# One engine program for the first layer's recurrence and its output product, the last head written out, and VectorE's key norm moved ahead in the second layer's first steps

## The chip, the cores and the metric

The kernel runs on one core of a Trainium2 chip. The time is the device time of one execution in microseconds (us), and shorter is better. Three runs of the kernel before took 2409.99, 2412.68 and 2415.59 us, so their median is 2412.68 us. The engines are TensorE (PE; the loading of its weights is listed apart as PEld), VectorE (DVE), ScalarE (ACT), GpSimd (POOL) and SyncE (SP), which here only issues transfers.

## The reference, cut to what matters

Three layers follow one another on x of 1024 rows by 1024 columns, all in float32: a retention layer, a window attention layer and a layer of two attention branches. The change touches the first layer and the first steps of the second.

```python
def retention_layer(x, g_norm, w_in, w_out, sin, cos):
    proj = rmsnorm(x, g_norm) @ w_in
    q, k, v, gate = jnp.split(proj, [...], axis=-1)      # 4 heads, q and k 256 wide, v and gate 512 wide
    q, k = theta_shift(q, sin, cos), theta_shift(k, sin, cos)
    o = rms(retention(q, k, v))                          # 8 chunks of 128 rows, a state carried from one to the next
    o = o.reshape(b, s, RET_V_TOTAL) * jax.nn.silu(gate) # 1024 x 2048
    return x + o @ w_out                                 # 2048 x 1024

def shared_kv(x, g_norm, w_kv, g_k):                     # head of the second layer
    kv = rmsnorm(x, g_norm) @ w_kv                       # 1024 x 256
    k, v = jnp.split(kv, [KV_WIDTH], axis=-1)
    k = rmsnorm(k, g_k)                                  # by head of 64
```

## The kernel before, in words

Rows are worked in 8 tiles of 128 (index t). Every large product is made of three TensorE matmuls, because each float32 operand is split into a high part (written by ACT) and a low part (the rest, written by DVE): high by high, low by high, high by low. So a product over 1024 rows of weights and 512 columns is 24 matmuls of 128x512, and a block of weights can be used only once ACT and DVE have split it. There is no planner: each engine's order is written out by hand, an engine works its own list from top to bottom, and semaphores join the lists. A wait holds up all that stands behind it in the same list.

**`retain` (L195).** After a preamble that makes the transposed normed rows hT, a loop on each engine (`Fori`) runs over the 4 heads. In each head there are three passes over the 8 tiles: queries with keys, values, gates. The third pass (the `for t in range(TILES)` in each engine's program) also does the recurrence: TensorE transposes the tile's queries and keys (L376), makes half of the gate product, the scores, the state's increment, the second half of the gate product, and last the tile's output into bank `p_o` (L275). ACT takes the square sum of that output (L507), POOL its power (L325), DVE multiplies output, factor and gate into `o_gated` (L652), and ACT stores these 128x512 rows to `ret_o_dram` (L455). While heads run, `w_raw` (the memory of `early_w_kv`) takes the next half block of weights and ACT and DVE split it (L420, L521) into `w_first` (one pair for each pass) or `w_second` (shared). At the end of the last head, this brings in the first block of the output weights: its upper half is split after tile 4, the lower half after tile 7.

**`retention_product` (L659).** It is a `Block` of its own, with memory, banks and semaphores of its own, entered once all engines have left `retain` and its semaphores are cleared. It loads the 2048 wide rows of tile t back from `ret_o_dram` (tile 0 to `o_rows`, tile 1 to `o_second`, which is the memory of `x_rows`; L712), transposes them in 16 pieces on TensorE (`transpose_rows`, L763), splits them in four steps on ACT (L808) and DVE (L850) to `oT`, and multiplies (`product(t, half)`, L780, 48 matmuls). It needs four blocks of output weights in the order of use: the one that `retain` left, one through `raw` (2 MB, L713, k of 0 to 7 for the left half of the columns), one in two halves through `raw_half` (1 MB each, L714 and L721, k of 8 to 15 for the right half), one through `raw` again (L719). ACT (L800) and DVE (L864) split them in this order, counted in `w_lo`. TensorE's list begins so:

```python
            transpose_rows(0)
            transpose_rows(1)
            for t in range(0, TILES, 2):
                product(t, 0)
                product(t + 1, 0)
                product(t, 1)
```

Here `product(0, 0)` waits for `w_lo` of 8 before its k of 0, and `product(0, 1)` for 16 at its start and 24 before its k of 0. DVE adds the product to the rows of x (L857).

**`window_layer` (L885), its first steps.** TensorE works in steps s: `rows(s)` transposes the rows of a tile (L1107), `keys_values(s - 1)` makes keys and values of the tile before (24 matmuls of 128x256), `transpose_keys(s - 2)` transposes the normed keys (L1122), which `norm_keys` on DVE has written to `kn` (L1426). DVE's list for a step is: `norm_low(s)` (two low parts of hT, L1411), `scale_rows(s + 3)` (rows times their factor, L1400, which waits for their load), `norm_keys(s - 2)`, `key_squares(s - 1)` (L1421), in steps 0 to 3 two `split_low` (L1417) and one `flip_bias` (L1405). Between `key_squares` and `norm_keys` of a tile lie a small ACT instruction (L1267) and POOL's power (L1068).

## Time and profile before

| | |
|---|---|
| median of three runs | 2412.68 us (2409.99 to 2415.59) |
| the profiled execution | 2418.01 us, of which the span of instructions is 2416.2 us |
| instructions | 33085 |
| share of the span: DVE, ACT, POOL busy | 46%, 37%, 9% |
| mean granted clock of TensorE | 0.976 of full speed |

The retention layer's heads run to 702 us of the span, the output product to 912 us and the second layer's key steps to some 970 us. Times in the rows are microseconds from the span's start. A busy share near 100% on one engine says that this engine is never without work in that stretch; an idle time stands in brackets with what ended it. The granted clock is the share of full speed at which TensorE was let run.

### The profile page before, as it was taken

The page shows a single profiled execution, that of the slowest core. Times are in us where ns is not written, and L with a number is a line of the kernel's source. Part 1 is how long each engine was busy: PE and PEld are TensorE (multiplying, and loading weights), DVE is VectorE, ACT ScalarE, POOL GpSimd, SP SyncE. Part 2 cuts the span into 40 slices and gives each one's busy share as a digit, 9 for nine tenths or more (in the row PEclk, how much of TensorE's full clock was granted, in tenths as well). Part 3 has the DMA queues.
Part 4 walks back from the last instruction along what each step waited for, and adds up shares of the span by engine and source line. Part 5 has one row for each costly group of instructions (what it writes and reads, how often), then busy time and mean ns, then how long its engine had stood idle before and what let it go on. Part 6 is the DMA issues. An engine that isn't in the chain of part 4 may idle for free. (4 is left out here: it accounts for less than half of the span.)

```text
span 2416.2 us, 33085 instructions
## 1 busy us (share of the span) xinstructions
PE 2281.6 (94%) x11898; PEld 1829.1 (76%) x11898; DVE 1116.9 (46%) x3122; ACT 885.2 (37%) x2276; POOL 212.3 (9%) x315
## 2 busy tenths in 40 slices
PE   6999999999979998999989799999999999799998
PEld 5888888888867887677767686777777777688876
DVE  5255264253453124445453316566665766533342
ACT  4142242341343113455543214454544544423232
POOL 1000000000000000112110000010010101101013
PEclk9999999999989999999999899999999999899999
DMA  4111111111136113011133501110111102424322
GB/s 142 38 53 52 54 56 50 56 48 54 48 132 220 70 61 114 10 49 51 49 109 107 171 34 58 60 43 8 60 43 60 44 7 77 131 73 122 96 96 87
DMA packets 125284, 174.95 MB, mean 72 GB/s; under 512 B 7576, under 2 KB 73176, under 8 KB 123616
## 3 DMA queue, kind: packets, MB, share of 16 engines
q1 hardware_dynamic: 119088, 157.39, 19.8%
q10 hardware_dynamic: 6064, 15.84, 1.8%
q8 instruction: 78, 1.28, 0.2%
q14 instruction: 54, 0.44, 0.1%
HBM read 143.79 MB, written 29.42 MB: 72 GB/s over the span
## 5 line engine op out<-in xcount | busy, mean ns | idle before, releaser
L91 PE MATMUL heads_p_ps<-ret_w_second_hi_sb,ret_hT_hi_sb 128*128 128x512 f32 x384 | 150.8, 393 | 1.8 <-DVE ret_w_second_lo_sb L521 1.8
L91 PE MATMUL heads_p_ps<-ret_w_second_lo_sb,ret_hT_hi_sb 128*128 128x512 f32 x384 | 149.8, 390 | 0.0
L91 PE MATMUL heads_p_ps<-ret_w_second_hi_sb,ret_hT_lo_sb 128*128 128x512 f32 x384 | 149.4, 389 | 0.0
L91 PE MATMUL att_proj_ps<-br_w_second_hi_sb,br_hT_hi_sb 128*128 128x512 f32 x272 | 117.3, 431 | 2.8 <-DVE br_w_second_lo_sb L2193 2.8
L2149 ACT ACTIVATE br_x_sb<-br_x_sb,att_max_neg_sb 128x256 f32<-128x256 f32 (+7 forms) x128 | 97.8, 767 | 27.4 <-DVE att_max_neg_sb L2366 27.3
L91 PE MATMUL att_proj_ps<-br_w_second_lo_sb,br_hT_hi_sb 128*128 128x512 f32 x272 | 107.1, 394 | 0.0
L91 PE MATMUL att_proj_ps<-br_w_second_hi_sb,br_hT_lo_sb 128*128 128x512 f32 x272 | 106.8, 392 | 0.0
L91 PEld LDWEIGHTS heads_p_ps<-ret_w_second_hi_sb,ret_hT_hi_sb 128*128 128x128 f32 x384 | 72.1, 188 | 18.8 <-issue 3.9
L2635 ACT ACTIVATE mrg_yT_hi_sb<-br_y_raw_sb 128x1024 fp32r<-128x1024 f32 x32 | 33.9, 1060 | 140.6 <-PE mrg_b_ps L2566 120.2
L91 PEld LDWEIGHTS heads_p_ps<-ret_w_second_lo_sb,ret_hT_hi_sb 128*128 128x128 f32 x384 | 72.1, 188 | 15.6
L91 PEld LDWEIGHTS heads_p_ps<-ret_w_second_hi_sb,ret_hT_lo_sb 128*128 128x128 f32 x384 | 72.2, 188 | 15.2
L2566 PE MATMUL mrg_b_ps<-mrg_w_br_hi_sb,mrg_yT_hi_sb 128*128 128x256 f32 x256 | 74.1, 289 | 9.6 <-DVE mrg_w_br_lo_sb L2727 8.1
L91 PE MATMUL swa_p_ps<-swa_w_first_hi_sb,swa_hT_hi_sb 128*128 128x512 f32 x160 | 70.9, 443 | 10.5 <-DVE swa_qn_sb L1441 7.0
L1974 PEld LDWEIGHTS att_t_ps<-all_ident_sb,br_x_sb 128*128 128x128 f32 x432 | 47.4, 141 | 41.2 <-DVE br_x_sb L2383 20.4
L1974 PE MATMUL att_t_ps<-all_ident_sb,br_x_sb 128*128 128x128 f32 x432 | 66.6, 281 | 9.5 <-DVE br_x_sb L2383 7.8
L420 ACT ACTIVATE ret_w_second_hi_sb<-early_w_kv_sb 128x512 fp32r<-128x512 f32 x52 | 28.5, 621 | 126.7 <-PE heads_p_ps L91 126.7
L2749 DVE TENSOR_TENSOR mrg_sig_sb<-mrg_b_ps,mrg_sig_sb 128x512 f32<-128x512 f32 x32 | 22.1, 689 | 113.2 <-PE mrg_b_ps L2566 113.2
L325 POOL TENSOR_TENSOR heads_o_rstd_sb<-heads_o_ms_sb,heads_minus_half_sb 128x1 f32<-128x1 f32 x32 | 17.6, 551 | 645.6 <-ACT heads_o_ms_sb L509 645.6
L2566 PE MATMUL mrg_b_ps<-mrg_w_br_lo_sb,mrg_yT_hi_sb 128*128 128x256 f32 x256 | 73.3, 286 | 0.0
L2566 PE MATMUL mrg_b_ps<-mrg_w_br_hi_sb,mrg_yT_lo_sb 128*128 128x256 f32 x256 | 73.2, 286 | 0.0
L857 DVE TENSOR_TENSOR early_x_rows_sb<-ret_out_y_ps,early_x_rows_sb 128x512 f32<-128x512 f32 x16 | 10.9, 688 | 129.8 <-PE ret_out_y_ps L780 129.8
L479 ACT ACTIVATE heads_v_sb<-heads_p_ps 128x512 f32<-128x512 f32 x32 | 19.2, 598 | 140.2 <-PE heads_p_ps L91 140.1
(472 smaller groups left out, 6553.0 us busy)
## 6 DMA issues: line engine op xcount, KB each, us to landing
early_w_kv_sb<-a_w_blocks SPq DMA_DIRECT2D x28, 1024.0 KB, 5.3
all_w_block_sb<-w_turns SPq DMA_DIRECT2D x12, 2048.0 KB, 9.0
br_y_raw_sb<-branch_yT_dram SPq DMA_DIRECT2D x32, 512.0 KB, 4.0
ret_o_dram<-early_x_rows_sb ACTq DMA_DIRECT2D x32, 256.0 KB, 2.4
all_w_block_sb<-swa_turns SPq DMA_DIRECT2D x4, 2048.0 KB, 9.6
ret_out_o_rows_sb<-ret_o_dram ACTq DMA_DIRECT2D x6, 1024.0 KB, 6.0
x_dram<-early_x_rows_sb SPq DMA_DIRECT2D x12, 512.0 KB, 2.8
heads_v_sb<-x SPq DMA_DIRECT2D x8, 512.0 KB, 4.6
```

What stands on the lines that cost most here:

```text
L91: mm = pe.matmul(out, rows[a], w[b], start=(k == 0 and a + b == 0), stop=(k == KT - 1 and b == 1))
L325: pool.tensor_tensor(o_rstd[:, t % 2:t % 2 + 1], o_ms[:, t % 2:t % 2 + 1], minus_half[:], ALU.pow).then_inc(orstd_done, 1)
L420: act.activation(w_at(kind)(k)[0], w_raw[:, k % HALF, :], ACT.Copy).then_inc(w_hi, 1)
L479: act.activation(v[:, t, :], p_proj[t % 2][:], ACT.Copy).then_inc(v_copied, 1)
L857: dve.tensor_tensor(x_rows[:, t % 2, cols], p_y[t % 2][half][:], x_rows[:, t % 2, cols], ALU.add).then_inc(x_added, 1)
L1974: tr = pe.transpose(p_tr[b][:, j * P:(j + 1) * P], probs[:, t % 2, a, (lo + j) * P:(lo + j + 1) * P], ident[:])
L2149: act.activation(part, part, ACT.Exp, bias=max_neg[:, t % 2, a:a + 1], scale=SCALE, accum_out=p_sum[:, t % 2, a:a + 1]).then_inc(exp_done, 1)
L2566: mm = pe.matmul(p_br[b][:, n * QW:(n + 1) * QW], rows[i], w[j], start=(k + i + j == 0), stop=(k == PAIRS - 1 and j == 1))
L2635: act.activation(y_parts[t % 2][0][:], y_raw[:, t % RAWS], ACT.Copy).then_inc(y_hi, 1)
L2749: dve.tensor_tensor(sig[:, t % 2, :], p_br[t % 2][:], sig[:, t % 2, :], ALU.mult).then_inc(prod_done, 1)
```

## The change

It has two parts.

**One program for recurrence and product.** `retention_product` makes no block, banks or memory of its own any more. It returns one function for each engine, and `retain` calls them behind its heads. The loop over heads covers three heads, and the last is written out:

```diff
+        def last_heads(eng, body):
+            with eng.Fori(0, RET_HEADS - 1) as h:
+                body(Place(h, 1, 0))
+            body(Place(None, 0, RET_HEADS - 1))
...
+            last_heads(pe, head_pe)
+            out["pe"](pe)
```

In the last head's last tile the transposes of the product's tile 0 stand inside the recurrence, two quarters at a time, with the ACT and DVE parts that belong to them:

```diff
                     mm.then_inc(s_done, 1)
+                    if last and t == TILES - 1:
+                        out["pe_ahead"](pe, 0)
...
                     project(2, t, range(HALF, KT))
+                    if last and t == TILES - 1:
+                        out["pe_ahead"](pe, 1)
...
-                pe.wait_ge(gate_done, head.times(TILES, TILES))
+                if not last:
+                    pe.wait_ge(gate_done, head.times(TILES, TILES))
```

ACT's first part (`act_ahead`, 0) stands after its split of the decayed queries, the second after the gate of tile 7 and the store of tile 6. DVE's (`dve_ahead`) stands right before the wait of the last `gated`. In the last head ACT and DVE no longer wait for all stores of `o_gated`.

SP's list behind the last head, where each load waits for the recurrence's own semaphores. `rows_stored` is the store of the tile's rows for all four heads; `first_rows_free` is the output of tile 3 of the last head, `second_rows_free` the last value product; `raw_free` is the transposes of tile 7; `raw_half_free` is the recurrence's last split; `gated_free` is that all rows are stored:

```diff
+    def sync_program(sp):
+        for t, place, free in ((0, o_rows, "first_rows_free"), (1, o_second, "second_rows_free")):
+            frees["rows_stored"](sp, t)
+            frees[free](sp)
+            sp.dma_start(place[:], o_dram[t * P:(t + 1) * P, :]).then_inc(o_first[t], 16)
+        frees["raw_free"](sp)
+        sp.dma_start(raw[:], dram["a_w_blocks"][FIRST + 2].rearrange("(k p) n -> p k n", p=P)).then_inc(raw_in, 16)
+        frees["raw_half_free"](sp)
+        sp.dma_start(raw_half, weight_rows(dram, FIRST + 1, 0)).then_inc(half_in, 16)
+        frees["gated_free"](sp)
+        for t in range(2):
+            sp.dma_start(x_rows[:, t], dram["x"][0, t * P:(t + 1) * P, :]).then_inc(x_in[t], 16)
+        sp.wait_ge(w_lo, KT)
...
```

TensorE's order in the product begins anew (`order` is k of 8 to 15, then 0 to 7), and the transposes go through the banks of `p_o0`, `p_kv0`, `p_kv1`, `p_p0` in the order 2, 3, 0, 1:

```diff
-            transpose_rows(0)
-            transpose_rows(1)
-            for t in range(0, TILES, 2):
+        product(0, 0, order[0:HALF])
+        transpose_rows(pe, 1)
+        product(0, 0, order[HALF:KT])
+        product(1, 0, order[0:KT])
+        product(0, 0, order[KT:])
+        product(1, 0, order[KT:])
+        for t in range(0, TILES, 2):
+            if t:
                 product(t, 0)
                 product(t + 1, 0)
```

ACT's list behind the last head is the load of tile 2's rows, the copies of tile 1, then the 24 splits; DVE's is the low parts of tile 1, then the 24 splits. From `product(0, 1)` on, the lists are those of before. The buffers of the product now lie over buffers of the recurrence (`o_rows` over the first half of v, `o_second` over `w_v_lo`, `oT` over v, the queries and keys, `spare` and the state), for which the buffers of `retain` are put in another order; `x_more` and `w_kv_high` lie over `v_high`.

**DVE's order in the second layer's first steps.**

```diff
             for s in range(TILES + 2):
+                if s >= 2:
+                    norm_keys(s - 2)
                 if s < TILES:
                     norm_low(s)
-                if s + 3 < TILES:
-                    scale_rows(s + 3)
-                if s >= 2:
-                    norm_keys(s - 2)
+                if s == 0:
+                    scale_rows(3)
                 if 1 <= s <= TILES:
                     key_squares(s - 1)
+                if 2 <= s < TILES - 2:
+                    scale_rows(s + 2)
```

## Rows read from the trace of the kernel before

**Rows 1.** The page, busy time of an engine (share of the span) and its instructions

```profile
PE 2281.6 (94%) x11898; PEld 1829.1 (76%) x11898; DVE 1116.9 (46%) x3122; ACT 885.2 (37%) x2276; POOL 212.3 (9%) x315
```

**Rows 2.** Busy time by stretch: length, each engine's busy us (instructions), granted clock, DMA share, GB/s

```profile
592.00:702.00 110.00, 109.81 (x512) 90.43 (x511) 48.95 (x101) 41.27 (x93) 3.86 (x7) 1.00 0.13 45
702.00:722.00 20.00, 6.84 (x31) 6.05 (x30) 6.75 (x11) 6.61 (x13) 0.65 (x2) 0.58 0.64 235
722.00:750.00 28.00, 24.91 (x105) 20.18 (x104) 15.87 (x27) 13.84 (x26) 0.00 (x0) 0.94 0.60 218
750.00:912.00 162.00, 162.00 (x766) 135.47 (x764) 29.91 (x51) 22.91 (x46) 6.05 (x14) 1.00 0.28 101
917.00:975.00 58.00, 48.14 (x320) 44.33 (x319) 27.71 (x52) 22.17 (x60) 6.46 (x9) 0.91 0.33 110
```

**Rows 3.** Timeline of TensorE, 702 to 750 us: start, length, instruction [idle before]

```profile
702.03 0.39 PE L275 MATMUL heads_o_ps<-heads_state_lo_sb,heads_qdT_hi_sb 128*128 128x512 f32 x1
...
714.08 3.68 PE L763 MATMUL ret_out_t_ps<-all_ident_sb,ret_out_o_rows_sb 128*128 128x128 f32 x16 [11.65 <-DMA ret_out_o_rows_sb<-ret_o_dram]
719.26 3.31 PE L763 MATMUL ret_out_t_ps<-all_ident_sb,early_x_rows_sb 128*128 128x128 f32 x16 [1.50 <-DVE ret_out_oT_lo_sb L850]
722.32 0.47 PE L780 MATMUL ret_out_y_ps<-ret_w_qk_hi_sb,ret_out_oT_hi_sb 128*128 128x512 f32 x1
...
731.13 0.50 PE L780 MATMUL ret_out_y_ps<-ret_hT_hi_sb,ret_out_oT_hi_sb 128*128 128x512 f32 x1 [3.09 <-DVE ret_hT_lo_sb L864]
...
749.18 0.39 PE L780 MATMUL ret_out_y_ps<-ret_w_v_hi_sb,ret_out_oT_hi_sb 128*128 128x512 f32 x1
```

**Rows 4.** Timeline of the other engines' lists, 680 to 745 us

```profile
680.75 0.37 SPq L306 DMA_DIRECT2D early_w_kv_sb<-a_w_blocks  x1
...
704.04 0.75 DVE L652 SCALAR_TENSOR_TENSOR early_x_rows_sb<-heads_o_ps,heads_o_rstd_sb,heads_gate_sb 128x512 f32<-128x512 f32 x1 [5.51 <-POOL heads_o_rstd_sb L325]
704.71 2.49 DVE L521 TENSOR_TENSOR ret_w_second_lo_sb<-early_w_kv_sb,ret_w_second_hi_sb 128x512 fp32r<-128x512 f32 x4
...
709.54 0.43 SPq L713 DMA_DIRECT2D all_w_block_sb<-a_w_blocks  x1
...
726.17 4.91 DVE L864 TENSOR_TENSOR ret_hT_lo_sb<-all_w_block_sb,ret_hT_hi_sb 128x512 fp32r<-128x512 f32 x8 [2.16 <-ACT ret_hT_hi_sb L800]
...
731.11 0.38 SPq L719 DMA_DIRECT2D all_w_block_sb<-a_w_blocks  x1
733.52 0.38 SPq L721 DMA_DIRECT2D early_w_kv_sb<-a_w_blocks  x1
...
742.63 2.19 ACT L800 ACTIVATE ret_w_gate_hi_sb<-early_w_kv_sb 128x512 fp32r<-128x512 f32 x4 [10.76 <-DMA early_w_kv_sb<-a_w_blocks]
```

**Rows 5.** The tile of the product's transposes: duration ns min/median/max, first and last start

```profile
L850 DVE TENSOR_TENSOR ret_out_oT_lo_sb<-ret_out_t_ps,ret_out_oT_hi_sb x32: 681/681/693, 715.9 to 870.0; 128x512 fp32r<-128x512 f32 x32
```

**Rows 6.** The chain that ended last: start, length of 24 matmuls 512 and 256 wide

```profile
2140.20 5.49 PE mrg_g_ps L91 x24
2145.70 2.88 PE mrg_b_ps L2566 x24
```

**Rows 7.** Timeline of DVE, POOL and TensorE in the second layer's first steps

```profile
925.28 0.75 DVE L1400 TENSOR_SCALAR ret_out_x_more_sb<-ret_out_x_more_sb,early_rstd_sb 128x1024 f32<-128x1024 f32 x1 [1.34 <-DMA ret_out_x_more_sb<-x_dram]
...
926.62 0.70 POOL L1068 TENSOR_TENSOR swa_k_rstd_sb<-swa_k_ms_sb,swa_minus_half_sb 128x2 f32<-128x2 f32 x1 [9.80 <-ACT swa_k_ms_sb L1267]
...
929.05 1.28 DVE L1411 TENSOR_TENSOR swa_hT_lo_sb<-swa_s_ps,swa_hT_hi_sb 128x512 fp32r<-128x512 f32 x2
...
930.90 0.42 DVE L1426 TENSOR_TENSOR swa_kn_sb<-swa_o_ps,swa_k_rstd_sb 128x256 f32<-128x256 f32 x1
...
931.38 0.69 PE L1122 MATMUL swa_o_ps<-all_ident_sb,swa_kn_sb 128*128 128x128 f32 x2 [4.29 <-DVE swa_kn_sb L1426]
...
953.82 1.04 PE L1107 MATMUL swa_s_ps<-all_ident_sb,early_x_rows_sb 128*128 128x128 f32 x8
```

**Rows 8.** Busy time by stretch, as in rows 2, behind the wait for the first keys

```profile
934.00:936.00 2.00, 2.00 (x12) 2.00 (x11) 2.00 (x4) 0.41 (x1) 0.00 (x0) 0.50 0.58 188
```

More of the change, by code:

```diff
@@ L265, in w_at @@
+        banks = dict(tr=[p_p0, p_o0, p_kv0, p_kv1], y=[[p_tr, p_s], [p_p1, p_o1]])
+        out = retention_product(nc, mem, layer, ident, dram, early, hT, w_first, w_second, o_dram, banks, frees, minus_half)
         def w_at(kind):
@@ L493, in _ @@
                         act.activation(qdT[0][:, b], qkT[:, b, 0:2], ACT.Copy).then_inc(qd_hi, 1)
+                    if last and t == TILES - 1:
+                        out["act_ahead"](act, 0)
                     if t + 1 < TILES:
@@ L505, in _ @@
                         store_rows(t - 1)
+                    if last and t == TILES - 1:
+                        out["act_ahead"](act, 1)
                     act.wait_ge(o_done, head.times(TILES, t + 1))
@@ L513, in _ @@
                 store_rows(TILES - 1)
-            for b in range(2):
-                act.wait_ge(o_out[b], 16 * RET_HEADS * TILES // 2)
+            last_heads(act, head_act)
+            out["act"](act)
         @block.vector
@@ L656, in _, with retention_product @@
                 split_next(2, 1)
-                for b in range(2):
-                    dve.wait_ge(o_out[b], head.times(16 * TILES // 2, 16 * TILES // 2))
-def retention_product(nc, ident, dram, early, hT, w_first, w_second, o_dram):
+                if not last:
+                    for b in range(2):
+                        dve.wait_ge(o_out[b], head.times(16 * TILES // 2, 16 * TILES // 2))
+            last_heads(dve, head_dve)
+            out["dve"](dve)
+def retention_product(nc, mem, layer, ident, dram, early, hT, w_first, w_second, o_dram, banks, frees, minus_half):
     HALF = KT // 2
@@ new lines, in retention_product @@
+    raw = early["w_q0"]
+    raw_half = early["w_kv"][:].rearrange("p k n -> p (k n)").rearrange("p (k n) -> p k n", n=BANK)
+    o_rows = mem.over("v", "o_rows", P, RET_HEADS * RET_V)
+    o_second = layer.over("w_v_lo", "o_second", P, RET_HEADS * RET_V)
+    oT = [[mem.over("spare", "oT0_hi", P, KO, P, dt=F32R), mem.over("state", "oT0_lo", P, KO, P, dt=F32R)],
+          [mem.over("v", "oT1_hi", P, KO, P, dt=F32R, further=4 * RET_HEADS * RET_V), mem.over("qkT", "oT1_lo", P, KO, P, dt=F32R)]]
@@ L769, in product, with pe_ahead, pe_program @@
+    def pe_ahead(pe, part):
+        transpose_rows(pe, 0, ORDER[2 * part:2 * part + 2])
+    def pe_program(pe):
+        order = list(range(KT, KO)) + list(range(KT))
+        def product(t, half, ks=order):
+            if ks[0] == KT:
+                pe.wait_ge(oT_lo, 4 * t + (4 if t else 2))
                 if t >= 2:
                     pe.wait_ge(x_added, 2 * (t - 2) + half + 1)
-                for n, k in enumerate(order):
-                    if t == 0 and half == 0 and k == 0:
-                        pe.wait_ge(w_lo, KT)
-                    if t == 0 and half == 1 and n == 0:
-                        pe.wait_ge(w_lo, 2 * KT)
-                    if t == 0 and half == 1 and k == 0:
-                        pe.wait_ge(w_lo, 3 * KT)
-                    w = w_at(k, half)
-                    for a, b in ((0, 0), (1, 0), (0, 1)):
-                        mm = pe.matmul(p_y[t % 2][half][:], oT[t % 2][a][:, k, :], w[b],
-                                       start=(n == 0 and a + b == 0), stop=(n == KO - 1 and b == 1))
@@ L782, in product @@
-                mm.then_inc(y_done[half], 1)
-            transpose_rows(0)
-            transpose_rows(1)
-            for t in range(0, TILES, 2):
+                else:
+                    frees["bank_free"](pe, t, half)
+            for k in ks:
+                if t == 0 and half == 0 and k in (KT, KT + HALF):
+                    frees["early_w"](pe, HALF if k == KT else KT)
+                if t == 0 and half == 0 and k == 0:
+                    pe.wait_ge(oT_lo, 4)
+                    pe.wait_ge(w_lo, KT)
+                if t == 0 and half == 1 and k == KT:
+                    pe.wait_ge(w_lo, 2 * KT)
+                if t == 0 and half == 1 and k == 0:
+                    pe.wait_ge(w_lo, 3 * KT)
+                w = w_at(k, half)
+                for a, b in ((0, 0), (1, 0), (0, 1)):
+                    mm = pe.matmul(p_y[t % 2][half][:], oT[t % 2][a][:, k, :], w[b],
+                                   start=(k == KT and a + b == 0), stop=(k == KT - 1 and b == 1))
```

417 lines of the change are left out of this document (224 added, 193 removed).

## The prediction

> **What bounds the kernel now.** The page's busy times come first: TensorE is busy 2281.6 us of the span, 94% [rows 1], so what can be won is mostly its idle time and the time at half clock. The busy time by stretch says where these are [rows 2]. In the last head TensorE is busy 109.81 of 110 us at full clock, and in the steady product 162.00 of 162. Between them, from 702 to 722 us, it is busy 6.84 of 20 at a granted clock of 0.58, and from 722 to 750 24.91 of 28 at 0.94. In the second layer's first steps it is busy 48.14 of 58 at 0.91. The change works on these holes only.
>
> The timeline of TensorE shows the first hole from within [rows 3]. The recurrence's last matmul starts at 702.03, the rows' transposes only at 714.08, ended by the load of rows, and the first product matmul at 722.32. Both sets of 16 transposes run cold, at 3.68 and 3.31 us. A second wait of 3.09 us ends at 731.13 with the split of the third weight block, and `product(0, 1)` starts at 749.18. The other lists say why [rows 4]: behind the last split (704.71 and 2.49 us) all engines leave the program, SP issues the 2 MB of `raw` at 709.54, and its split on DVE starts at 726.17. In the second layer [rows 7] TensorE waits 4.29 us, until 931.38, for keys that DVE writes at 930.90, though POOL had their factor at 927.3 (926.62 and 0.70); behind that wait the clock is 0.50 [rows 8].
>
> **Part one: the seam.** I walk TensorE's new list in the clock of before. 24 matmuls 512 wide take 5.49 us at full clock [rows 6], so 12 take 2.75. Sixteen transposes take 3.68 us at half clock [rows 3]; at full clock I take half, 1.84.
>
> - The tile 0 transposes now stand inside the last tile of the last head and add 1.84 us. What they wait for is early: SP comes to the row loads right behind its last weight load, at 681.1 (680.75 and 0.37) [rows 4], some 16 us before the first transpose. The last recurrence matmul moves from 702.03 to 703.9, and all that hangs on it moves with it: the last split on DVE ends at 704.71 + 2.49 + 1.84 = 709.05 [rows 3, 4].
> - 704.1: `product(0, 0)` with k of 8 to 11, 2.75, to 706.85. Its low parts came from DVE while the gate product ran. Then tile 1's transposes, 1.84, to 708.7. Their rows were loaded with the first.
> - k of 12 to 15 need the last split, 709.05: a wait of 0.4. To 711.85.
> - `product(1, 0)` with k of 8 to 15 needs tile 1's low parts: four on DVE at 0.68 [rows 5], which overlap as four splits in 2.49 do [rows 4], done at 711.55. No wait. To 717.35.
> - `product(0, 0)` with k of 0 to 7 needs eight splits from `raw`: DVE starts them at 711.55 and takes 4.91 [rows 4], to 716.45. The load is now issued when tile 7's transposes are done, near 694.5, instead of at 709.54; even with the 16.0 us that it took before (to 725.5, by DVE's 726.17 less one ACT split) it lands at 710.5. No wait. To 722.85, and `product(1, 0)` with k of 0 to 7 to 728.35.
> - `product(0, 1)` needs the second half of the fourth block. SP issues the second `raw` and then this half when `w_lo` allows, the first at 716.45. Before, from the first issue (731.11) to ACT's start on the half (742.63) went 11.52 us, with 3 MB in flight [rows 4]. The same again gives 727.95, then four ACT splits at 2.19 and the last DVE part at 0.68: 730.85. So TensorE, at 728.35, waits 2.5 us.
>
> This wait is new. Before, the half's DVE part was done at 742.63 + 2.19 + 0.68 = 745.5 for a start at 749.18, with 3.7 us to spare: the weight chain takes the place of the seam as what is late. `product(0, 1)` starts at 730.85 instead of 749.18: **18.3 us less**. From there the lists are those of before and run at 162 of 162 [rows 2]. The barrier at the product's end stays, with one set of semaphores to clear instead of two; nothing for it.
>
> Bounds: without the new wait the gain is 749.18 - 728.35 = 20.8. If loads of rows, x and `raw_half`, which now start within 3 us of one another, stretch the pair's 11.52 us to the 16.0 of the first crowded load, 4.5 more are lost, and the half clock behind such a wait costs up to (1 - 0.94) x 28 = 1.7 [rows 2]. That leaves 12.1. I take 18.3, as the chain of 11.52 us is the same two loads. A wait that the new lists add, with what stands behind it: ACT and DVE have the tile 0 copies ahead of the last square sum and the last `gated`; ACT was idle there, and DVE was idle 5.51 us before `gated` [rows 4]. SP's wait for `raw_half_free` holds the loads of x, which DVE needs only after its 24 splits.
>
> The Trainium skill ("TensorE: Matmul & The Clock Gate", Part 1) says that "the default state is throttled, and activity releases the throttle", so that idle time can bring 1.2 GHz back. The wait of 3.09 us [rows 3] lies in the stretch with clock 0.94 [rows 2] and agrees; for a wait of 2.5 us the sum by this rule would be 18.3 less up to 1.7, by mine 18.3.
>
> The written-out head itself: three loop rounds and straight code replace four rounds. TensorE's work in it is the same, and ACT, DVE and SP compute no addresses there. I take nothing, as the product, straight code already, runs 162 of 162 us [rows 2].
>
> **Part two: the keys.** In step 2 DVE now writes `kn` before `norm_low` and `scale_rows`, so by the order alone at 929.05 instead of 930.90, 1.85 earlier [rows 7]. More comes from step 1: `scale_rows(4)`, with its wait of 1.34 for a load and 0.67 of work at 925.28, is gone from it, and with it the wait ahead of `key_squares(0)`. ACT's and POOL's small steps and the two splits follow some 2 us sooner, and `kn` is started near 927.2, just as TensorE comes free (931.38 - 4.29 = 927.1). I keep 0.5 of the 4.29 as DVE's 0.42 with its hand-over: 3.8 gained. Behind it TensorE stays at full clock. Before, one transposed tile and one keys-and-values product ran cold or partly so: at full clock the product is 2.88 [rows 6] and eight transposes are half of 1.84; at half clock twice as much, so up to 3.8 more, of which I take 2.5, since the clock came back before the product's end. The step after was late as well and is caught up by the same order; against this DVE's splits and flips in steps 2 and 3, now between two `norm_keys`, leave TensorE waits that I put at 0.6 a step. I walked the lists up to `rows(6)`: 947.7 instead of 953.82 [rows 7], **6.1 us less**, waits and clock together. `scale_rows(s + 2)` one step later harms nothing: it is still a step ahead of the transposes that need it.
>
> Bounds: 1.85 (the order alone, nothing earlier in step 1, clock as before), and 8 (all waits of three steps and all cold time). Below nothing: `norm_keys` now holds up `norm_low` where POOL's factor is late; its part is 0.70 a tile [rows 7], so a loss of 1 to 2 if that happened in the two PE-bound steps too.
>
> **The sum.** 18.3 + 6.1 = 24.4 us. Against the profiled execution, 2418.0 (span 2416.2), that is 2393.6. The median of the three runs is 5.3 below the profiled one, and what is taken away is engine time that both have: 2412.7 - 24.4 = 2388.3 us.
>
> **The rivals.**
>
> 1. *The weight chain takes more of it back.* The loads of tile 2's rows, of `raw_half` and of x (3 MB) start just ahead of the pair. For it: the first `raw` took 16 us in a crowd of 5 MB; against it: that load is now issued 15 us sooner and out of the crowd. At the lower bound, 12.1 + 6.1, the time is 2394.5. Chance 0.17.
> 2. *No new wait.* The second half is issued later behind `raw` than before, so the pair may need less than 11.52 us from its first issue only if the loads overlap better. 20.8 + 7 gives 2385. Chance 0.17.
> 3. *The key order yields its least.* DVE's list is then bound by ACT's part in each step, and the wait comes back one step on. 18.3 + 1.85 gives 2392.5. Chance 0.12.
> 4. *Slower: instruction fetch in the written-out head.* Five engines now run new code where a loop ran. If each came late with its code where the transfers are crowded, TensorE would stop again and again. It decides only when it exceeds 24.4 us over a head of some 164 us; the price at twice that is 2437, and at the point where it balances the gain the time is 2413. Against it: the straight product at 162 of 162 us, through stretches of DMA load. Chance 0.03.
> 5. *The change doesn't do what it says*: the rows for the inner transposes land late or a wait on the recurrence's semaphores is reached only at its end, so that little but the program exit is saved, at most from the last split's end at 707.2 to `raw`'s issue at 709.54 [rows 4]. 2.3 + 6.1 gives 2404. Chance 0.05.
>
> The Trainium skill ("Runtime: NRT & Kernel Launch", Instruction fetch mechanics) says that the sequencer fetches the next page by itself while it executes the current one, and that a taken branch to a page outside its window forces a fetch first. By that, rival 4 would not come, and one taken branch fewer would be a small gain; here the boundaries between the looped heads cost TensorE nothing that the last head's 109.81 of 110 us would show, so that gain is nothing too.
>
> **How the numbers follow.** The forecast has 0.46. Rivals 1, 3 and 5 reach up, 2 down. The range of 8 in 10 runs from 2382 (rival 2 and the key part's upper bound) to 2400 (rivals 1 and 3 together: 12.1 + 1.85 gives 2398.8). Within 0.2% (4.8 us, about what a measurement of this kernel can tell from no change) would need the gain to fall below 4.8, which only rivals 4 and 5 near their ends give: 0.03. Slower: 0.03. Faster: 0.94.
>
> **What would show it.** After the last recurrence matmul the next product matmul follows within 0.3 us; tile 0's transposes stand before it at full clock; the granted clock from 702 to 730 is 1.00. `product(0, 1)` starts some 27 us behind the last recurrence matmul (47.2 before), with a wait of 2 to 3 us on the split of `w_gate`. If the wait is absent, rival 2; if it is longer than 4, rival 1. The wait for `kn` is under 1 us, the clock behind it 1.00, and `rows(6)` comes 6 us nearer to the second layer's first transposes. The prediction fails if TensorE shows idle time inside the last head, or if the stretch from `product(0, 1)` on takes longer than before.

## The result and the profile after

The changed kernel took 2397.38 us (median of four runs, 2396.69 to 2401.20) where the kernel before, on the same chip, took 2414.14 (2409.99 to 2417.85). The ratio is 0.9934, with a 95% interval of 0.9914 to 0.9954: 11 to 21 us faster. The forecast was 2388.3 in a range of 2382 to 2400. The time lies in it, near its upper end. The profiled execution took 2397.63 us, its span is 2395.8 us, 20.4 less than the one of before.

The page, with TensorE's busy time against [rows 1], and the busy time by stretch against [rows 2]; the columns are the same:

```profile
PE 2277.5 (95%) x11898; PEld 1827.9 (76%) x11898; DVE 1116.7 (47%) x3122; ACT 881.5 (37%) x2274; POOL 212.6 (9%) x314
```

```profile
592.00:702.00 110.00, 109.77 (x523) 91.15 (x522) 51.54 (x105) 41.62 (x96) 3.85 (x7) 1.00 0.23 84
702.00:722.00 20.00, 19.65 (x95) 16.28 (x94) 12.86 (x21) 11.39 (x23) 0.55 (x1) 1.00 0.81 279
722.00:750.00 28.00, 24.47 (x117) 20.20 (x116) 11.69 (x19) 9.45 (x18) 0.74 (x2) 1.00 0.59 204
...
898.00:956.00 58.00, 48.64 (x325) 44.67 (x327) 28.56 (x54) 23.13 (x63) 7.44 (x10) 0.91 0.34 109
```

The 20 us behind the heads, where TensorE was busy for 6.84 at a clock of 0.58, are now 19.65 at 1.00. The 58 us from the second layer's first transposes on are almost as before: 48.64 busy for 48.14, and the same 0.91. So the first part of the change did its work and the second did little. TensorE's timeline at the seam answers to [rows 3]:

```profile
701.80 0.39 PE L350 MATMUL heads_o_ps<-heads_state_lo_sb,heads_qdT_hi_sb 128*128 128x512 f32 x1
...
704.76 1.04 PE L857 MATMUL heads_kv_ps<-all_ident_sb,ret_o_second_sb 128*128 128x128 f32 x8
...
707.02 0.50 PE L886 MATMUL heads_tr_ps<-ret_w_second_hi_sb,heads_oT_hi_sb 128*128 128x512 f32 x1 [0.35 <-DVE ret_w_second_lo_sb L613]
...
729.90 0.47 PE L886 MATMUL heads_s_ps<-ret_w_v_hi_sb,heads_oT_hi_sb 128*128 128x512 f32 x1 [3.53 <-DVE ret_w_gate_lo_sb L987]
```

`product(0, 1)` starts at 729.90 instead of 749.18. The wait of 11.65 us for rows is gone, and what stands in its place is a wait of 3.53 us for the second half of the fourth weight block. The other engines' lists, for [rows 4], say where that half is held up:

```profile
707.00 0.38 SPq L810 DMA_DIRECT2D early_w_kv_sb<-a_w_blocks  x1
708.00 1.06 SPq L813 DMA_DIRECT2D early_x_rows_sb<-x  x2
714.20 0.38 SPq L815 DMA_DIRECT2D all_w_block_sb<-a_w_blocks  x1
719.18 0.38 SPq L817 DMA_DIRECT2D early_w_kv_sb<-a_w_blocks  x1
...
715.99 2.20 ACT L924 ACTIVATE ret_w_v_hi_sb<-early_w_kv_sb 128x512 fp32r<-128x512 f32 x4 [4.26 <-DMA early_w_kv_sb<-a_w_blocks]
726.59 2.19 ACT L924 ACTIVATE ret_w_gate_hi_sb<-early_w_kv_sb 128x512 fp32r<-128x512 f32 x4 [8.40 <-DMA early_w_kv_sb<-a_w_blocks]
```

From the issue of the second `raw` (714.20) to ACT's start on the second half (726.59) go 12.39 us; before it was 11.52. The first half had been split 10 us earlier, yet TensorE does not use it, because its one wait asks for both halves.

The second layer's first steps, against [rows 7]:

```profile
897.99 1.94 PE L1233 MATMUL swa_s_ps<-all_ident_sb,heads_x_more_sb 128*128 128x128 f32 x8 [4.81 <-PEq L137]
...
908.84 0.44 PE L1248 MATMUL swa_o_ps<-all_ident_sb,swa_kn_sb 128*128 128x128 f32 x2 [0.25 <-DVE swa_kn_sb L1552]
...
912.14 0.36 PE L91 MATMUL swa_o_ps<-heads_w_kv_high_sb,swa_hT_hi_sb 128*128 128x256 f32 x1 [1.99 <-ACT swa_k_all_sb L1397]
...
919.34 0.36 PE L91 MATMUL swa_m_ps<-heads_w_kv_high_sb,swa_hT_hi_sb 128*128 128x256 f32 x1 [1.51 <-ACT swa_k_all_sb L1397]
...
932.41 1.04 PE L1233 MATMUL swa_s_ps<-all_ident_sb,early_x_rows_sb 128*128 128x128 f32 x8
```

The wait for the normed keys fell from 4.29 to 0.25 us. Three microseconds on there is another, of 1.99 us, for a thing that the prediction does not mention: `k_all`, the copy of the transposed keys, which ACT writes. The trace of before already had a wait for it one product later, so a look at the next few waits would have found it:

```profile
940.78 0.36 PE L91 MATMUL swa_m_ps<-ret_out_w_kv_high_sb,swa_hT_hi_sb 128*128 128x256 f32 x1 [1.51 <-ACT swa_k_all_sb L1271]
```

ACT's list in the changed kernel shows what the copy stood behind:

```profile
908.80 0.27 ACT L1391 ACTIVATE swa_v_all_sb<-swa_m_ps 128x128 f32<-128x128 f32 x1
...
910.20 0.20 ACT L1393 ACTIVATE swa_k_ms_sb<-swa_k_ss_sb 128x2 f32<-128x2 f32 x1 [1.13 <-DVE swa_k_ss_sb L1547]
...
910.31 1.32 ACT L1385 ACTIVATE swa_w_second_hi_sb<-all_w_block_sb,early_norm_cols_sb 128x512 fp32r<-128x512 f32 x2
...
911.54 0.45 ACT L1397 ACTIVATE swa_k_all_sb<-swa_o_ps,early_norm_cols_sb 128x256 f32<-128x256 f32 x1
```

Behind that wait the clock is at half (0.50, the level of 1.2 GHz), as it was behind the old one [rows 8]:

```profile
914.00:916.00 2.00, 2.00 (x12) 2.00 (x11) 0.60 (x2) 0.00 (x0) 0.00 (x0) 0.50 0.23 82
```

From the first transposes to `rows(6)` it is 34.42 us (932.41 - 897.99), before 37.07 (953.82 - 916.75).

### The profile page after: what moved, and what is told of

Its sections match the earlier page's. It is cut to its first block and busy times, and to the rows that moved or that the text cites. A ratio compares the mean times of both kernels' runs of the same rounds, so it can differ in the third digit from the quotient of the medians.

```text
span 2395.8 us, 32894 instructions
## 1 busy us (share of the span) xinstructions
PE 2277.5 (95%) x11898; PEld 1827.9 (76%) x11898; DVE 1116.7 (47%) x3122; ACT 881.5 (37%) x2274; POOL 212.6 (9%) x314
## 5 line engine op out<-in xcount | busy, mean ns | idle before, releaser
L1994 POOL TENSOR_TENSOR att_o_pow_sb<-att_o_ms_sb,att_minus_half_sb 128x2 f32<-128x2 f32 x32 | 31.6, 986 | 416.1 <-ACT att_o_ms_sb L2259 416.1
```

The costliest lines, as they stand in the source:

```text
L1994: pool.tensor_tensor(o_pow[:], o_ms[:], minus_half[:], ALU.pow).then_inc(opow_done, 1)
```

## Experiments

Every kernel was compared with the kernel before on its own chip in five rounds, so the ratios, rather than the times, compare kernels of different chips. "Stretch A" is from the last recurrence matmul to the transposes of the product's tile 2, "stretch B" from the second layer's first transposes to `rows(6)`, both in the profiled execution.

**The changed kernel again**, with no edit.

> The changed kernel once more, for a narrow ratio. Its profile was 20.4 us shorter in span than that of before, but the medians of four runs only 16.8 apart, because the profiled execution of before was one of the slow ones of 2410 to 2418. Theory A (the gain is engine time at three places, 2.1 in the heads, 17.2 at the seam, 2 in the key steps): ratio near 0.992, 19 to 21 us. Theory B (part of it was only the profile's state of the clock): 15 to 17 us, ratio near 0.9935.

2397.54 us (five runs), ratio 0.9928 [0.9915, 0.9941]. The last recurrence matmul starts at 701.33, stretch B is 34.37, and the wait in front of `product(0, 1)` is 3.93 us. One thing differs from the first profile: behind this wait the clock fell.

```profile
730.00:732.00 2.00, 2.00 (x5) 1.63 (x6) 2.00 (x4) 2.00 (x5) 0.00 (x0) 0.50 0.00 0
732.00:734.00 2.00, 2.00 (x8) 1.56 (x8) 2.00 (x5) 0.88 (x2) 0.00 (x0) 0.76 0.00 0
```

The 48 matmuls of `product(0, 1)` take 12.43 us here (729.84 to 742.27) and 11.00 in the first profile (729.90 to 740.90), so the first profile flatters the change by 1.4 us. The gain by the ratio, 17.4 us, lies between the two theories, under the 20.4 of the two profiles.

**The key order alone**, on the kernel before: the second part's diff and nothing else.

> Kernel before with DVE's new order of the key steps alone. By the two traces the stretch from the second layer's first transposes to rows(6) went from 37.1 to 34.4 us, so 2.7 us less is expected (ratio 0.999), with the wait for kn of 4.29 us gone, a wait for ACT's copy of the keys of some 2 us in its place, and the clock at one half behind it. Rival (my prediction): 6.1 us, clock 1.00, if the wait for the copy was an accident of the one execution.

2414.27 us, ratio 0.9997 [0.9988, 1.0006]: nothing that can be measured. Stretch B is 34.20 us (915.16 to 949.36), 2.9 less than in the first profile of before, with waits of 0.34, 1.99 and 1.51 us and the half clock behind the second, as expected. The rival of 6.1 us is refuted.

**The seam alone**: the changed kernel with the old order in DVE's list.

```diff
+                if s + 3 < TILES:
+                    scale_rows(s + 3)
+                if s >= 2:
+                    norm_keys(s - 2)
...
-                if 2 <= s < TILES - 2:
-                    scale_rows(s + 2)
```

> Changed kernel with DVE's old order of the key steps: the seam, the written-out head and the new order of memory without the second part. Expected 17 to 19 us less than before (ratio 0.9925 to 0.993), and 37 us again from the first transposes to rows(6). If the parts interact (the key steps meet other transfers), the sum of this run's gain and that of the keys alone misses the whole by more than 2 us.

2398.02 us, ratio 0.993 [0.9917, 0.9944], the time of the whole change. Stretch B is 35.77 us (899.05 to 934.82) with the wait for the keys back at 3.52. So in the time the gain is the seam's. The key order is worth 1.4 us here and 2.9 in the run above; over all profiles, stretch B is 35.8 to 37.8 us in the four with the old order and 34.2 to 34.8 in the six with the new one (without the copy moved below), so 2.3 us in the mean, too little for these runs to tell in the time.

**The placement alone**: the kernel before with two small buffers put behind the large ones. In before they lie between `v_high` and `sin`, so that here `sin`, the queries, keys, gates, scores and the state move, while v and its parts stay. In the changed kernel they lie near the end.

```diff
-        g_col = mem.sb("g_col", P, KT)
-        tab = mem.sb("tab", P, RET_TAB)
...
         state_parts = mem.parts("state", P, 2, RET_V)
+        g_col = mem.sb("g_col", P, KT)
+        tab = mem.sb("tab", P, RET_TAB)
```

> Kernel before in which only g_col and tab (32 and 1032 bytes a partition) are allocated behind the state's parts instead of ahead of sin, so that all tensors of the recurrence stand at other addresses; nothing else. Theory: the 432 matmuls of heads_kv and heads_o take 389 to 391 ns in the changed kernel instead of 393 to 398 because of the place of their operands; then here as well, and the last recurrence matmul starts some 2 us sooner than 702.03, at 700. Rival: it is the constant waits and addresses of the written-out head or the shorter loop; then nothing changes here.

2413.51 us, ratio 0.9992 [0.9983, 1.0002]. In the time it is not shown, but the trace shows it. One line of the recurrence's matmuls in the kernel before and then in this one; duration in ns (least, median, most), then first and last start:

```profile
L275 PE MATMUL heads_kv_ps<-heads_v_high_sb,heads_k_dec_lo_sb x56: 394/394/394, 136.0 to 688.5; 128*128 128x512 f32 x56
```

```profile
L275 PE MATMUL heads_kv_ps<-heads_v_high_sb,heads_k_dec_lo_sb x56: 387/390/395, 136.8 to 687.0; 128*128 128x512 f32 x56
```

The heads took 552.5 us from the first to the last of these and take 550.2 now, 2.3 less, with nothing changed but where the buffers lie. The changed kernel has the same 550.2 (136.4 to 686.6). The other profiles of each order agree within 0.2 us, and the last recurrence matmul starts at 700.42, as expected. This line went from 394 to 390 ns in the median; of the recurrence's other matmuls one group went only from 390 to 389, and those of v with the scores from 393 to 398 down to 389. Why, the runs do not show.

**The copy of the keys earlier on ACT**, on the changed kernel.

```diff
             def keys_values(t):
...
+                if t >= 1:
+                    copy_keys(t - 1)
                 act.wait_ge(kss_done, t + 1)
...
-                if s >= 3:
-                    copy_keys(s - 3)
+                if s == TILES + 2:
+                    copy_keys(TILES - 1)
```

> The changed kernel with one instruction of ACT moved: the flipped-sign-free copy of the keys of tile t-1 (to k_all) stands ahead of the wait for the key squares of tile t instead of at the head of the next step but one. Theory A (the wait that took the place of the one for kn is this copy, which stood in ACT's list behind two high splits and a small step that waits for DVE): the wait of 1.99 us ahead of the third keys-and-values product goes to under 0.3 us, the clock behind it stays 1.00, the waits of 1.51 us and 1.16 us for the same buffer go as well, and the stretch from the second layer's first transposes to the transposes of tile 6 falls from 34.4 us to 30 to 32. In the time 2 to 4.5 us less than the changed kernel, about 2394. Theory B (the copy is only the last of several things that come together, so another wait takes over, for a high or low part of hT or for kn): the copy's waits go and the stretch stays at 33.5 us or more; time within 1 us of the changed kernel.

2396.70 us (2391.24 to 2397.54), ratio 0.9916 [0.9901, 0.9931]. Stretch B is 30.46 us (900.50 to 930.96), 4.0 less, and all waits for `k_all` up to `rows(6)` are gone:

```profile
911.85 0.44 PE L1248 MATMUL swa_o_ps<-all_ident_sb,swa_kn_sb 128*128 128x128 f32 x2 [0.23 <-DVE swa_kn_sb L1554]
...
916.49 0.44 PE L1248 MATMUL swa_m_ps<-all_ident_sb,swa_kn_sb 128*128 128x128 f32 x2 [0.34 <-DVE swa_kn_sb L1554]
...
921.11 0.44 PE L1248 MATMUL swa_o_ps<-all_ident_sb,swa_kn_sb 128*128 128x128 f32 x2 [0.34 <-DVE swa_kn_sb L1554]
```

Theory A holds in the trace. In the time it is blurred: two of the five runs took 2391.2 and 2391.4 us, three 2396.7 to 2397.5. The profiled one is of the upper three, and its stretch A is 41.86 us, the longest of the six with this wait of the changed kernel, by the clock behind it: 0.50 from 729 to 735.

**The rows of x later on SP**, on the changed kernel: the two loads behind the second half block instead of ahead of the second `raw`.

```diff
-        frees["gated_free"](sp)
-        for t in range(2):
-            sp.dma_start(x_rows[:, t], dram["x"][0, t * P:(t + 1) * P, :]).then_inc(x_in[t], 16)
         sp.wait_ge(w_lo, KT)
...
         sp.dma_start(raw_half, weight_rows(dram, FIRST + 1, 1)).then_inc(half_in, 16)
+        frees["gated_free"](sp)
+        for t in range(2):
+            sp.dma_start(x_rows[:, t], dram["x"][0, t * P:(t + 1) * P, :]).then_inc(x_in[t], 16)
```

> The changed kernel with the two loads of the rows of x (1 MB together) issued by SP behind the second load of raw and the second half block, instead of ahead of them. Theory A (the wait of 3.3 to 3.9 us ahead of product(0, 1) is long because the first half block shares the DMA engines with the rows of x: the half, issued at 707.0, lands only at 715.9): the half lands at 712 to 713, DVE's 24th split ends 2 to 3 us sooner, the wait falls to 0.5 to 1.5 us and the clock behind it stays 1.00; 2 to 3 us less than the changed kernel where that clock was 1.00, up to 4 where it was not; time about 2395. Theory B (the half block is late because of what is in flight before it, rows of tile 2 and the first raw, or the chain is set by the second half alone, whose own load and splits take 11.5 us from the issue of the second raw): the wait stays above 2.5 us; time within 1 us. Against the edit in either theory: the additions of x come at 720 and later, so a load that lands after 735 would hold DVE.

2397.95 us, ratio 0.993 [0.9916, 0.9943]. The first half did land early (ACT starts on it at 713.44 instead of 715.99), the second did not, and the wait is 3.33 us:

```profile
713.64 0.37 SPq L812 DMA_DIRECT2D all_w_block_sb<-a_w_blocks  x1
716.63 0.37 SPq L814 DMA_DIRECT2D early_w_kv_sb<-a_w_blocks  x1
...
725.83 2.19 ACT L924 ACTIVATE ret_w_gate_hi_sb<-early_w_kv_sb 128x512 fp32r<-128x512 f32 x4 [10.19 <-DMA early_w_kv_sb<-a_w_blocks]
```

The half was issued 2.6 us sooner and came as late: 12.19 us from the issue of the second `raw`, as 12.39 in the changed kernel. Theory B holds: what sets the end is the pair of 3 MB that begins with the second `raw`. That the rows of x delayed the first half is not shown either: with them ahead of it, ACT starts on the half at 713.76 to 714.26 in four other profiles (the seam alone, the earlier copy, the last two below), and with both edits together, where they stand behind it, only at 716.47.

**Both edits together.**

> Both edits of the two runs before together: the copy of the keys earlier on ACT and the rows of x later on SP. If both theories A hold, the savings lie 170 us apart on TensorE's path and add up: 4 to 8 us less than the changed kernel, about 2391, and 0.9 to 1.1% less than the kernel before (ratio about 0.990). If the two theories B hold it stays at 2397.

2393.37 us, ratio 0.9908 [0.9893, 0.9924]: 4 us less than the changed kernel. Stretch B is 30.05 us (900.37 to 930.42), as with the key copy alone, and stretch A is 41.21, so the rows of x gave nothing.

**Nothing inside the head**: tile 0's transposes and their ACT and DVE parts right behind the heads.

```diff
             last_heads(pe, head_pe)
+            out["pe_ahead"](pe, 0)
+            out["pe_ahead"](pe, 1)
             out["pe"](pe)
```

> The changed kernel with the transposes of the product's tile 0 and their ACT and DVE parts placed right behind the last head instead of inside its last tile; everything else (one program, no exit, early loads, new order of k) as changed. Theory A (the gain is that the engines do not leave the program, so that the loads start early and the chain of weights runs ahead; the interleaving only fills): the recurrence ends 1.9 us sooner, TensorE then waits 2 to 3 us for the copies of tile 0, and DVE's four low parts of tile 0 delay the 24 weight splits by under 3 us, so that product(0, 1) starts 0 to 3 us later than in the changed kernel (730 to 733) and the time is 0 to 3 us above it. Theory B (standing inside the head is what hides the transposes): product(0, 1) starts 5 us or more later, and the time is 5 to 8 us above the changed kernel.

2402.79 us, ratio 0.9956 [0.9943, 0.997], 5.3 us above the changed kernel. The recurrence ends 2.1 us sooner, and then:

```profile
706.15 0.80 PE L881 MATMUL heads_tr_ps<-ret_w_qk_hi_sb,heads_oT_hi_sb 128*128 128x512 f32 x1 [4.28 <-DVE heads_oT_lo_sb L962]
711.43 1.31 PE L852 MATMUL heads_kv_ps<-all_ident_sb,ret_o_second_sb 128*128 128x128 f32 x8
...
735.10 0.47 PE L881 MATMUL heads_s_ps<-ret_w_v_hi_sb,heads_oT_hi_sb 128*128 128x512 f32 x1 [2.39 <-DVE ret_w_gate_lo_sb L982]
```

The first wait is 4.28 us and costs the clock (0.50 from 706 to 711); tile 1's transposes come 6.7 us later, and DVE's and ACT's weight splits stand behind their copies. The second `raw` is issued at 720.43 instead of 714.20, and the whole chain moves by that: `product(0, 1)` starts at 735.10. Theory B holds, in the time and in the start. Of some 17 us that the change is worth, one program (with the new placement) brings about 12 and the interleaving about 5. TensorE alone would have come to `product(0, 1)` at 732.71 instead of 726.37, and the weight chain, held up in the lists of ACT and DVE, adds its wait of 2.39 us; the chain is what ends last, so it sets the 5 us. How the 12 us divide over the missing exit, the earlier load of `raw` (issued at 692.15 in this run, at 709.54 in the kernel before) and the new order of k, no run shows.

**The wait of `product(0, 1)` divided**, on the changed kernel. The first 12 matmuls use the first half block only.

```diff
-                if t == 0 and half == 1 and k == KT:
-                    pe.wait_ge(w_lo, 2 * KT)
+                if t == 0 and half == 1 and k in (KT, KT + HALF):
+                    pe.wait_ge(w_lo, KT + HALF if k == KT else 2 * KT)
```

> The changed kernel with one wait of TensorE divided: product(0, 1) starts when the first half of the right block is split (w_lo of 12, at 719.2) and waits for the second half (w_lo of 16) only ahead of its k of 12. Theory A (the 3.3 to 4.1 us of idle time ahead of product(0, 1) is one wait put too early, while its first 12 matmuls had their weights 10 us before; the idle time is also what lets the clock fall, by 0 to 2.6 us in one execution or another): product(0, 1) starts at 726.1 to 726.8, a wait of 0.3 to 1.3 us stands behind its 12th matmul, the clock stays 1.00 there, and from the end of product(1, 0) to the second layer's first transposes it is 2.75 us shorter than in the best of the executions seen and up to 5 shorter than in the worst; time 2.7 to 4.5 us less than the changed kernel, about 2394. Theory B (a wait later in the same chain, for the second raw block at k of 0, takes its place, as its splits end at 734.5 and the matmuls now come to it 2.7 us sooner, near 732.5): the first wait goes, one of about 2 us appears at k of 0, and the time is within 1 us of the changed kernel.

2395.89 us, ratio 0.9917 [0.9903, 0.9930]. `product(0, 1)` runs on at 725.88, but the idle time comes back in two pieces:

```profile
730.34 0.50 PE L886 MATMUL heads_s_ps<-ret_w_gate_hi_sb,heads_oT_hi_sb 128*128 128x512 f32 x1 [1.57 <-DVE ret_w_gate_lo_sb L987]
...
735.15 0.50 PE L886 MATMUL heads_s_ps<-ret_hT_hi_sb,heads_oT_hi_sb 128*128 128x512 f32 x1 [1.80 <-DVE ret_hT_lo_sb L987]
```

The sum is 3.37 us, as theory B has it, since the last block's splits end where they did. The clock is 1.00 behind both pieces, and stretch A is 39.30 us, against 40.94 in the second profile of the changed kernel. So neither theory is whole: the idle time stayed, its cost in clock went. Against the first profile of the changed kernel, with 39.10 us at clock 1.00, nothing is gained, and the time is 1.6 us less, within the spread of these runs. The clock is 1.00 at the seam in all three profiles with the divided wait and in one of the six where the whole wait stands, 3.3 to 4.1 us.

**The divided wait and the earlier copy of the keys.**

> The changed kernel with the divided wait of the run before and the earlier copy of the keys on ACT. The copy of the keys shortened the stretch from the second layer's first transposes to those of tile 6 from 34.4 to 30.5 us; the divided wait is worth 2.7 to 4.5 us if theory A of the run before holds. Sum 6.5 to 8.5 us less than the changed kernel's 2397.5: 2389 to 2391, ratio to before about 0.990. If theory B of that run holds, 2393.5 (the copy alone).

2388.78 us (2387.50 to 2390.45), ratio 0.989 [0.9875, 0.9906], just below the 2389 to 2391 expected. Stretch A is 37.56 us, stretch B 30.05 (896.01 to 926.06). At the seam only the wait at k of 0 is left, 1.76 us. The first of the two pieces is absent because ACT starts on the second half at 725.31 instead of 727.12; nothing that this run adds to the one before touches that load.

**The last wait of `product(0, 1)` divided by k as well.**

```diff
-                if t == 0 and half == 1 and k == 0:
-                    pe.wait_ge(w_lo, 3 * KT)
+                if t == 0 and half == 1 and k < KT:
+                    pe.wait_ge(w_lo, 2 * KT + k + 1)
```

> The kernel of the run before last (divided wait, earlier copy of the keys) with the last wait of product(0, 1) divided too: instead of all 24 splits ahead of its k of 0, TensorE waits for one split more ahead of each k. DVE makes one low part in 0.6 us (eight in 4.89), TensorE uses one k in 0.68 us, so once the first part is there TensorE should never catch up. Theory A (what is left of the idle time at the seam is the coarseness of the waits): the wait of 1.76 us at k of 0 falls to under 0.3 us, unless the second raw block itself lands late, and the time is 1.5 to 2 us less than 2388.8, about 2387. Theory B (what follows is bound elsewhere, for instance by the rows of x or the addition behind product(0, 1)): no change within 1 us.

2388.28 us (2386.68 to 2392.03), ratio 0.989 [0.9873, 0.9906]. TensorE's waits at the seam are down to the old 0.35 us, and stretch A is 35.66 us (701.76 to 737.42), 1.9 less, as theory A says; in the median 0.5, within the spread. These last two are the fastest versions, 27 to 28 us under before and 9 under the changed kernel.

**The kernel before again.**

> The kernel before, once more, as a measure of what repetition alone does. Expected: a ratio of 1.000 within 0.001, a profile within 8 us of the first. If the profiled execution of before (2418.0) was high by chance, its second profile shows where: less time at half clock or in waits somewhere, the same durations and order otherwise. If its product(0, 1) follows the last recurrence matmul by 47 us again (749.18 less 702.03), the comparison of the seam stands as read from one execution.

2416.66 us (11 runs), ratio 1.0001 [0.9992, 1.0010]; the profiled span is 2414.9. `product(0, 1)` starts at 749.37, 47.08 us behind the last recurrence matmul (702.29), as in [rows 3]. But this is not the same in every execution. The runs of the key order alone and of the placement alone left the seam's code as it was, and there it is 44.49 and 44.75 us. The wait for the third weight block ends 28.0 and 28.3 us behind the last recurrence matmul instead of 29.1 and 29.0, and the clock behind it stays at 1.00 instead of falling to 0.50. This run and then the key order alone:

```profile
731.30 0.50 PE L780 MATMUL ret_out_y_ps<-ret_hT_hi_sb,ret_out_oT_hi_sb 128*128 128x512 f32 x1 [4.42 <-DVE ret_hT_lo_sb L864]
```

```profile
731.13 0.50 PE L780 MATMUL ret_out_y_ps<-ret_hT_hi_sb,ret_out_oT_hi_sb 128*128 128x512 f32 x1 [1.62 <-DVE ret_hT_lo_sb L864]
```

Stretch A is 58.03 and 57.96 us in the two profiles of before and 55.37 and 55.64 in those two. Stretch B is 36.44 us (916.94 to 953.38) and the wait for the keys 2.78 instead of 4.29: that wait depends on the execution as well.

## Why the prediction was right, and where it was not

- **The walk through the seam held.** Counted from the last recurrence matmul, k of 12 to 15 was to start at +5.15 us and started at +5.22 (707.02 - 701.80), with a wait of 0.35 for 0.4. `product(1, 0)` was to end at +24.45 and ended at +24.57. The second `raw` was to be issued at +12.55 and was at +12.40.
- **The new wait is real and was sized a little small**: 3.53 us (3.3 to 4.1 in five more executions) for 2.5. The pair took 12.39 us for 11.52, its splits the rest. The row of 11.52 has the second load issued 2.4 us behind the first; here it was 5.0, since the first half landed late, which "the same again" left out. Rival 2, no new wait, is refuted. Rival 1 (6.2 us more taken back) was right by 1.0 of them, and not by the crowd that it named: delaying the rows of x did not shorten the wait. Rival 5, little but the exit saved, falls with the start at 729.90.
- **The clock behind it** was taken at 1.00, with up to 1.7 us as a bound. The first profile agrees with 1.00. But in five other executions with the same wait (the repeated one, the seam alone, both edits apart and together) `product(0, 1)` took 12.43 to 13.61 us instead of 11.00, so 1.4 to 2.6 more, and the bound was too low. The rule that the prediction set beside its sum, that idle time can bring the low clock back (the Trainium skill, "TensorE: Matmul & The Clock Gate", Part 1), was the better guide: a wait of this length sometimes costs its clock and sometimes does not.
- **The transposes in the head** cost 1.9 us as taken (eight in 1.04 and twice four in 0.60, overlapping). Yet the recurrence ended 0.23 us before its old time, not 1.84 behind it. The term that was missed is 2.3 us of faster recurrence, from the buffers' new places (the placement run). It was luck for the forecast: without it `product(0, 1)` would have started 1.2 us after the 730.85 foreseen instead of 1.0 before it. "The buffers are put in another order" stood in the description and was given no price.
- **The written-out head**, taken as nothing, is nothing: the same 550.2 us looped (placement run) and written out (136.4 to 686.6). Rival 4 is refuted. The prediction's ground for a boundary between looped heads costing nothing was misread, though: the stretch from 592 to 702 us lies inside the last head, whose table is loaded at 573.21 us, and holds no such boundary. The claim holds all the same, as from 130 to 702 us TensorE's waits that the profile lists come to 1.8 us, none above 0.3.
- **The barrier** at the product's end was taken as unchanged. It costs 0.4 more, 4.79 to 4.81 us in every profile with one program against 4.41 to 4.42 in every profile with two.
- **The keys were the step that failed**: 6.1 us predicted, 2.65 found between the two first profiles, 1.4 and 2.9 with the order alone, 2.3 in the mean of all profiles. It did hold that the wait for `kn` would be under 1 us (0.25). What failed is "the clock behind it 1.00" and the walk up to `rows(6)`: `keys_values(2)` also waits for the copy of the keys, and in ACT's list this stood behind a wait for DVE and two splits. Rival 3 named about this size, 1.85, and nearly the place ("bound by ACT's part in each step"). The earlier copy gave 4.0 us more, so the sum the prediction had is there, once both waits are taken.
- **From the profile to the median.** The 5.3 us between the profiled execution of before and its median were taken off the forecast. The profiled execution of the changed kernel lies only 0.25 above its median, and over more runs before's median is 2414.5 to 2416.7, so 1.3 to 3.5 below its profile. Three runs were too few for this step. The two profiled executions also differ in luck at the seam, both in the change's favour: stretch A went from 58.03 to 39.10 us, 18.9 less, while four profiles with the old seam have 56.75 in the mean and four with the new one (the first two, the seam alone, the earlier copy) 40.60, 16.2 less. So these two profiles show 2 to 3 us more at the seam than it gives on average, most of it through the clock behind the waits.
- **The range** reached down to 2382. Its own ground, 20.8 + 8, gives 2383.9; nothing was added for the rest.

In sum, the forecast missed by 9.1 us (2397.4 less 2388.3). 5.1 of these are the step to the median (5.3 less 0.25). The other 4.0 lie between the two profiles: 3.4 at the keys (6.1 less 2.65), 0.5 at the barrier and the product's end (the first transposes came 18.8 us sooner, `product(0, 1)` 19.3), 1.0 behind `rows(6)` (21.4 sooner there, 20.4 at the end), and 1.0 back at the seam (19.3 for 18.3), where the faster recurrence gave 2.1 and the longer wait took 1.0.

## What to carry to other kernels

When an engine's wait is shortened, list every semaphore that the next few instructions wait on, and look up in the other engines' lists what stands ahead of each: a copy behind a wait and two splits took over here at once, and moving it ahead of them gave more than the reorder itself (4.0 us of stretch B against 2.3). A program boundary costs more than its barrier, since all that the next stage could have loaded, transposed and split ahead waits for it too. Where a wait asks for more of a chain than the next matmuls use, divide it: here this first saved no idle time, only the half clock behind it, and with one wait more divided the last 1.8 us of idle time went too. Before reading a seam from two traces, look whether the same code elsewhere in the series reads the same: here four traces of the old seam lie 2.7 us apart.

## What the runs showed of the hardware

- The places of the operands in SBUF change a matmul's time. With two small buffers moved and the same instructions in the same order, the medians of the recurrence's matmuls of 128x512 went from between 390 and 398 ns to between 389 and 393 (the first of each group of three into `heads_kv` apart, 438 to 435), 2.3 us over the heads.
- The clock does not follow from the length of a wait alone. Behind 3.53 us of idle time it stayed at 1.00 in one execution, and behind 3.33 us it fell to 0.50 in two others. Behind 1.57 and 1.80 us at the seam it stayed, behind 2.39 us there it fell, and behind 1.99 us at the keys it was 0.50 in all six profiles that have this wait. Ahead of the waits at the seam TensorE runs product matmuls, ahead of the 1.99 us it runs ten transposes (908.84 to 910.15 in the changed kernel); whether this matters, no run tests. What decides it is open.
- The two loads of 3 MB ahead of `product(0, 1)` took the longer, the later the second was issued, but not by all of it, and with a scatter of its own. From the first issue to ACT's start on the second went 11.4 to 12.1 us in five profiles with the second issued 2.4 us behind the first, 11.5 to 12.6 in five at 2.9 to 3.5, and 12.4 to 13.3 in four at 5.0 to 6.0.
